# Two-layer hybrid mixer on one core: HGRN's masks on ScalarE, branch outputs by features, modulation blocks under mLSTM's gates

## The reference

```python
mod = silu(c) @ w_mod[l] + b_mod[l]                 # shift, scale, gain; 24 column blocks
o_a = softmax attention of MLA
o_b = two-way gated linear attention (HGRN):  scores[t,s] = sum_k q[t,k] k[s,k] prod(f[s+1..t,k])
o_c = mLSTM, two-way, with exponential gates and a maximum for stability
o_d = retention: q, k turned by a rotary table, scores * gamma^|t-s|, two-way
outs = [o_a, rms_norm(o_b)*silu(g_b), rms_norm(o_c)*sigmoid(g_c), rms_norm(o_d)*silu(g_d)]
acc  = sum_n sigmoid(gate_n) * (outs[n] @ w_branch[n]);   x = x + g1 * (acc @ w_out)
x    = x + g2 * (relu(h @ w_ff1)**2 @ w_ff2)
```

## Time and profile before

| | us |
|---|---|
| three runs | 1765.21, 1768.84, 1768.99 (median 1768.84) |
| the profiled execution | 1768.83, its span 1767.0 |
| TensorE busy | 1639.5 (93%), 9934 matmul records |
| VectorE, ScalarE, POOL busy | 862.8, 688.5, 263.8 |
| mean granted TensorE clock | 0.965 of full |

### The profile page before, as it was taken

One profiled execution on the slowest core, in us unless ns is written; L12 is line 12 of the kernel. 1 busy time (PEld: TensorE's weight loads), 2 busy tenths in 40 slices (PEclk: granted clock), 3 DMA queues, 4 the chain that ended last, 5 costly groups with the idle time before them and its releaser, 6 DMA issues.

```text
span 1767.0 us, 23662 instructions
## 1 busy us (share of the span) xinstructions
PE 1639.5 (93%) x9934; PEld 1347.5 (76%) x9934; DVE 862.8 (49%) x1283; ACT 688.5 (39%) x970; POOL 263.8 (15%) x193
## 2 busy tenths in 40 slices
PE   5987899999999999889999999878899989989998
PEld 3776686775667768667777777677788777989998
DVE  4399425554363325532223223469456554566553
ACT  5510223343635423433113322350345466455452
POOL 0044001230121110022002200012002230203030
PEclk9998999999999999899999999888999999989999
DMA  8331233212221143244443444221231322445552
GB/s 337 109 130 49 73 126 113 93 74 65 85 78 60 55 155 108 83 167 167 167 157 139 157 167 143 85 88 45 95 128 69 123 76 94 146 149 201 181 191 96
DMA packets 36442, 213.02 MB, mean 121 GB/s; under 512 B 3888, under 2 KB 7344, under 8 KB 12656
## 3 DMA queue, kind: packets, MB, share of 16 engines
q1 hardware_dynamic: 36336, 211.50, 33.3%
HBM read 209.39 MB, written 2.10 MB: 120 GB/s over the span
## 4 chain that ended last, share of the span: by engine, by line
PE 81%; DVE 11%; ACT 5%; issue 2%; DMA 1%; SPq 0%; DVEq 0%; ACTq 0%
PE ps L971 10%; PE ps L973 9%; PE ps L972 9%; PE ps L527 9%; PE ps L529 8%; PE ps L528 8%; PE ps L505 5%; DVE arena L1785 5%; PE ps L772 3%; PE ps L582 2%; PE ps L802 2%; PE ps L841 2%; DVE parts L1627 2%; DVE arena L1754 1%; PE ps L638 1%
## 5 line engine op out<-in xcount | busy, mean ns | idle before, releaser
L527 PE MATMUL ps<-parts,whi 128*128 128x512 f32 (+1 forms) x928 | 334.0, 360 | 7.1 <-issue 3.0
L529 PE MATMUL ps<-parts 128*128 128x512 f32 (+1 forms) x960 | 331.2, 345 | 0.0
L973 PE MATMUL ps<-parts 128*128 128x512 f32 (+1 forms) x960 | 323.3, 337 | 0.0
L528 PE MATMUL ps<-parts,whi 128*128 128x512 f32 (+1 forms) x928 | 320.7, 346 | 0.0
L971 PE MATMUL ps<-parts 128*128 128x512 f32 (+1 forms) x928 | 315.0, 339 | 0.0
L972 PE MATMUL ps<-parts 128*128 128x512 f32 (+1 forms) x928 | 312.5, 337 | 0.0
L1653 DVE TENSOR_TENSOR parts<-ring,parts 128x1024 fp32r<-128x1024 f32 x124 | 147.6, 1232 | 248.8 <-ACT parts L1246 248.8
L1627 DVE TENSOR_TENSOR parts<-ring,whi 128x1024 fp32r<-128x1024 f32 (+1 forms) x136 | 174.1, 1322 | 134.3 <-ACT whi L1216 134.2
L1246 ACT ACTIVATE parts<-ring 128x1024 fp32r<-128x1024 f32 x124 | 124.4, 1050 | 264.0 <-PE ps L973 251.8
L1216 ACT ACTIVATE whi<-ring 128x1024 fp32r<-128x1024 f32 (+1 forms) x136 | 134.7, 1041 | 210.0 <-DMA ring<-in_w_in 98.0
L527 PEld LDWEIGHTS ps<-parts,whi 128*128 128x128 f32 x928 | 177.5, 191 | 43.2 <-issue 21.4
(11 more groups left out here) (255 smaller groups left out, 2221.0 us busy)
## 6 DMA issues: line engine op xcount, KB each, us to landing
ring<-in_w_ff SPq DMA_DIRECT2D x64, 1024.0 KB, 4.8
ring<-in_w_in SPq DMA_DIRECT2D x60, 1024.0 KB, 5.0
ring<-in_w_mod SPq DMA_DIRECT2D x40, 1024.0 KB, 4.8
arena<-in_w_mod SPq DMA_DIRECT2D x8, 1024.0 KB, 20.8
ring<-in_w_branch SPq DMA_DIRECT2D x32, 256.0 KB, 5.2
ring<-in_w_out SPq DMA_DIRECT2D x8, 1024.0 KB, 4.8
arena<-in_tables_rt SPq DMA_DIRECT2D x2, 1280.0 KB, 7.7
X<-in_x SPq DMA_DIRECT2D x2, 1024.0 KB, 7.8
```

The source lines that it names most:

```text
L527: pe.matmul(ps[0:m, 0:n], w_hi[:, k, c], x_hi[:, k, 0:n], start=(k == 0), stop=False)
L528: pe.matmul(ps[0:m, 0:n], w_hi[:, k, c], x_lo[:, k, 0:n], start=False, stop=False)
L529: last = pe.matmul(ps[0:m, 0:n], w_lo[:, k, c], x_hi[:, k, 0:n], start=False, stop=(k == KD - 1))
L973: last = pe.matmul(ps[:, 0:nt], w_lo[:, k, c], x_hi[:, k, 0:nt], start=False, stop=(k == kt - 1))
```

## The change

In layer 0 the modulation blocks that ran behind hg, mq, mk and mv run behind mLSTM's merge tiles; HGRN's gates take blocks 12 to 15 and mLSTM's 16 to 19, `PACKS` follows. mLSTM's 16 gate columns are loaded into the tail of mo's slot. POOL's `masks` go: ScalarE copies the wanted halves and writes zeros to the others. Queries of level 2L are scaled before the keys of level L. Values become weights (64 wide), scores move, heads 2j and 2j+1 go to the two halves of the columns, and the result has features in partitions; the norms of HGRN and retention are sums by a matrix of ones, Ln and Exp; MLA's sums are spread by products with the identity. mLSTM keeps the old way (`branch_tokens`). Retention works on pairs of heads, with one buffer for the backward decays (`RDB`), and its decays 2 and 3 move ahead on ScalarE and POOL. The products across 128 alternate between the halves of the rows.

The core of the diff:

```diff
-    return [("mod", 0, {HG: 16, MLA: 20}[n] + j)] if n in (HG, MLA) else []
...
-IN_EXTRA = ("hq", "hv", "hg", "mq", "mk", "mv", "rq", "rk")
...
-PACKS = [(0, 8, 8), (0, 16, 4), (0, 20, 4), (1, 0, 8), (1, 8, 8), (1, 16, 8)]
+    return [("mod", 0, {HG: 12, ML: 16, MLA: 20}[n] + j)] if n != RT else []
...
+IN_EXTRA = ("hq", "hv", "rq", "rk")
...
+PACKS = [(0, 8, 4), (0, 12, 8), (0, 20, 4), (1, 0, 8), (1, 8, 8), (1, 16, 8)]
...
-                return [(0, KD * (b - a), io["w_in"][l, :, KD * a:KD * b])]
+                last = [(2048, 2048 + KD * 16, io["w_in"][l, :, KD * b:KD * (b + 16)])] if key[2] == "mo" else []
+                return [(0, KD * (b - a), io["w_in"][l, :, KD * a:KD * b])] + last
...
-                    last.then_inc(*product.up(("o", HG, l, g)))
-
...
+                for j in range(2):
+                    ps = bank(("o", HG, l, j), fixed=j)
+                    for i in range(2 * rounds):
+                        for step in range(16 // (2 * rounds)):
+                            t, k = divmod(done, KD)
+                            if k == 0:
+                                pv = bank(("rv", l, t))
+                            value_step(l, "rv", t, k, pv)
+                            done += 1
+                        if i + j == 0:
+                            pe.wait_ge(*s_hx.at(("x256", l, 3)))
+                            pe.wait_ge(*s_hp.at(("pt", l, 64, 3 if l == 0 else 1)))
+                        other = i + 1 - 2 * (i % 2)
+                        blocks = [(PT[:, :, i, :], i), (XP1[:, :, other * P:(other + 1) * P], other)]
+                        if i < 2:
+                            blocks += [(XP2[:, :, s * 256 + i * P:s * 256 + (i + 1) * P], 2 + s) for s in range(2)]
+                        last = weigh_pair(ps[:, i * P:(i + 1) * P], j, blocks, HV)
+                    last.then_inc(*product.up(("o", HG, l, j)))
+
+            def weigh_pair(o, j, blocks, values):
+
+                for n, (scores, s) in enumerate(blocks):
+                    for e in range(2):
+                        h = 2 * j + e
+                        last = pe.matmul(o[64 * e:64 * e + 64], values[:, s, h * HD:(h + 1) * HD], scores[:, h],
+                                         start=(n == 0), stop=(n == len(blocks) - 1))
                 return last
+
+            def branch_sum(n, l, j):
+
+                nt = T if l == 0 else LAT
+                pe.wait_ge(*s_oa.at(("osq", n, l, j)))
+                ps = bank(("os", n, l, j))
+                for e in range(2):
+                    r = slice(64 * e, 64 * e + 64)
+                    last = pe.matmul(ps[r, 0:nt], tab("ones")[r, 0:64], SQ[r, j, 0:nt], start=True, stop=True)
+                last.then_inc(*product.up(("os", n, l, j)))
...
+            def retention_scores(l, j):
+
+                for b in range(3 if l == 0 else 2):
+                    pair = [bank(("rqk", l, 2 * j + e, b)) for e in range(2)]
+                    q0 = LAT if b == 2 else 0
+                    for i in range(2):
+                        s = i if b == 0 else 2 + i
+                        for e, ps in enumerate(pair):
+                            r = slice(64 * e, 64 * e + 64)
+                            last = pe.matmul(ps[:, i * 256:(i + 1) * 256], RK[r, j, s * P:(s + 1) * P], RQ[r, j, q0:q0 + LAT],
+                                             start=True, stop=True)
+                            if i:
+                                last.then_inc(*product.up(("rqk", l, 2 * j + e, b)))
...
-                            last.then_inc(*product.up(("ro", l, h)))
-                    mla_turn(l, *divmod(h, 2))
+                retention_scores(l, 0)
+                merge(l, ML, [6])
+                retention_values(l, 0)
+                for j in range(2):
+                    mla_turn(l, 1, j)
...
+            def mla_spread(l):
+
+                pe.wait_ge(*s_av.at(("asum", l)))
+                for j in range(2):
+                    ps = bank(("rb", l, j))
+                    for t in range(4 if l == 0 else 2):
+                        g, i = divmod(t, 2)
+                        for e in range(2):
+                            c = 4 * i + 2 * j + e
+                            last = pe.matmul(ps[64 * e:64 * e + 64, t * P:(t + 1) * P],
+                                             asum[:, g, c:c + 1].broadcast_to([P, HD]), tab("ident"), start=True, stop=True)
+                    last.then_inc(*product.up(("rb", l, j)))
...
-                for g in rounds:
-                    branch_turn(HG, l, g)
+                    if j == 0:
+                        for i in range(2):
+                            branch_sum(HG, l, i)
...
+            def mask_zeros(l, L):
+
+                i = LEVELS.index(L)
+                for g in range(2 if l == 0 else 1):
+                    if L > 2:
+                        act.wait_ge(*product.at(("hl", l, L // 4, 2 * g + 1)))
+                    for rows, side in ((FW, 0), (BW, 1)):
+                        v = halves(QS[i % 2], rows, g * LAT, (g + 1) * LAT, L, side)
+                        z = zero4[rows, 0:1].unsqueeze(2).broadcast_to([64, HEADS, P // L]) if L == 1 else \
+                            zero4[rows, 0:1].unsqueeze(2).unsqueeze(3).broadcast_to([64, HEADS, P // L, L])
+                        act.activation(v, z, ACT.Copy)
+
+            def mask(l, L):
+
+                i = LEVELS.index(L)
+                act.wait_ge(*s_hd.at(("decq", l, L)))
+                for g in range(2 if l == 0 else 1):
+                    for rows, side in ((FW, 1), (BW, 0)):
+                        v, q = [halves(x, rows, g * LAT, (g + 1) * LAT, L, side) for x in (QS[i % 2], QT)]
+                        last = act.activation(v, q, ACT.Copy)
...
+                    ps = read(act, ("o", n, l, j))
+                    act.activation(SQ[:, j, 0:nt], ps[:, 0:nt], ACT.Square, scale=HD ** -0.5)\
+                        .then_inc(*s_oa.up(("osq", n, l, j)))
+                if n == HG:
+                    part_high(l, ("gate", HG, 0))
+                for j in range(2):
+                    ps = read(act, ("os", n, l, j))
+                    freed(("os", n, l, j), "branch_raw", ("oln", n, l, j))
+                    act.activation(RS[:, j, 0:nt], ps[:, 0:nt], ACT.Ln, bias=tab("eps")).then_inc(*s_oa.up(("oln", n, l, j)))
+                for j in range(2):
+                    act.wait_ge(*s_oa.at(("oln", n, l, j)))
+                    act.activation(RS[:, j, 0:nt], RS[:, j, 0:nt], ACT.Exp, scale=-0.5).then_inc(*s_oa.up(("ort", n, l, j)))
...
-                elif h >= 2:
-                    act.wait_ge(*s_rv.at(("prob", l, h - 2)))
-                for d, far in enumerate((RADF, RADB)):
-                    act.activation(RD[h % 2][d], far, ACT.Exp, scale=lgam(l, d, h)).then_inc(*s_ra.up(("e", l, h, d)))
...
+                for d, (far, e) in enumerate(((RADF, RD[h]), (RADB, RDB))):
+                    if h and d:
+                        act.wait_ge(*s_rp.at(("d", l, h - 1)))
+                    act.activation(e, far, ACT.Exp, scale=lgam(l, d, h)).then_inc(*s_ra.up(("e", l, h, d)))
...
+                retention_decay(l, 2)
...
                         merge(l, ML, [2, 3])
...
+            def query_decay(l, L):
+
+                nq = T if l == 0 and L < 128 else LAT
                 if L < 128:
                     dve.wait_ge(*s_hm.at(("mask", l, L, 1 if l == 0 else 0)))
                 else:
                     dve.wait_ge(*product.at(("h128", l, 1, 1)))
...
+                dve.wait_ge(*s_hd.at(("decq", l, L)))
+                if L > 1:
+                    dve.wait_ge(*s_hd.at(("gate", l, L)))
+                scale(QT, FW, 0, nq, L, 1)
+                scale(QT, BW, 0, nq, L, 0).then_inc(*s_hd.up(("decq", l, 2 * L)))
+
+            def key_decay(l, L):
+
+                if L < 128:
+                    dve.wait_ge(*product.at(("hl", l, L, 3 if l == 0 else 1)))
                 if L > 1:
...
+                for j in range(2):
+                    dve.wait_ge(*s_oa.at(("ort", n, l, j)))
+                    freed(("o", n, l, j), "branch_normed", ("on", n, l, j))
+                    dve.scalar_tensor_tensor(out=RS[:, j, 0:nt], in0=bank_of(("o", n, l, j))[:, 0:nt], scalar=gain,
+                                             in1=RS[:, j, 0:nt], op0=ALU.mult, op1=ALU.mult)\
+                        .then_inc(*s_ov.up(("on", n, l, j)))
+                if n == HG:
+                    part_low(l, ("gate", n, 0))
+                for j in range(2):
+                    dve.wait_ge(*s_ov.at(("on", n, l, j)))
+                    dve.wait_ge(*s_pa.at((name, l, 1)))
+                    dve.tensor_tensor(OUT[:, n % 2, j, 0:nt], RS[:, j, 0:nt], gate[:, j, 0:nt], ALU.mult)\
+                        .then_inc(*s_og.up(("og", n, l, j)))
...
-                    if h:
-                        mla_turn(l, *divmod(h - 1, 2))
-                mla_turn(l, 1, 1)
+                merge(l, ML, [5])
+                for j in range(2):
```

(76 more changed lines are left out.)

341 lines of the change are left out of this document (140 added, 201 removed).

## The result

The changed kernel takes 1747.95 us (median of four runs, 1744.10 to 1750.91) against 1767.22 for the kernel before, a ratio of 0.9884 with a 95% interval of 0.9864 to 0.9903. So it is faster, by 1.2%, clear of the scatter: by 19 us in the medians and by 22.8 in the profiled executions (1746.02 against 1768.83, spans 1744.2 and 1767.0), where 53.8 were forecast. 1715.0 was wrong, and so was the range, which ended at 1740.

A forecast was written before the change was run, and what follows sets the result against it. TensorE, busy 93% of the span, was taken as the bound, with VectorE's scalings holding the ladder; gains of 56.0 less 2.2 for small tiles gave 53.8 off 1768.8, so 1715.0 us, range 1703 to 1740.

The forecast's parts named there:

- The ring's look-ahead: Under mLSTM's gates: loads shortened by the moved blocks cost nothing, over 8 us against loads of 4.8; blocks themselves -4.3 us.
- a wait for loads under mLSTM's gates: Listed sign that would make the forecast wrong, in mLSTM's stage; given no size.
- The ladder: HGRN's levels: masks off POOL end its slowing of VectorE's key scalings; 22.5 us gained in layer 0, 10.9 in layer 1.
- Values by features: Value products in overlapping half-array pairs: HGRN +7.8 us, retention and MLA +8.8 each before walking their stages.
- rival (b): Tiles don't overlap, so values, scores, sums and spread lose 42.2 us: 1757; chance 0.07.
- Branch sums: Norm sums by a matrix of ones, 5.2 us added; in layer 0 a pair takes 0.86 us.
- Rival (a): Sums' two row halves writing one bank run one after another, costing 5.2 us more: 1720; chance 0.12.
- New waits: HGRN's gates wait longer for a bank held until VectorE copies mLSTM's rows, -3.8 us; layer 1's mLSTM branch -3.2.
- the wait for decay 2: Layer 1: decay 2 with two table loads comes before gate 1's sigmoid on ScalarE, within a term of -3.2 us.
- Retention and MLA: Walked stages: first RT gate earlier by 7.8 us in layer 0 and 8.4 in layer 1; MLA +9.9.
- (c): More waits than walked, through ScalarE and the rotating banks: six stages each lose 2.5 us more, 1730; chance 0.08.

The follow-up runs named there:

- experiment 1: Changed kernel with modulation block 16 loaded and multiplied behind the second kv projection instead of behind mLSTM's gate block 0; 1725.88 us, ratio 0.9769.
- experiment 3: Kernel before with only the four modulation blocks moved out of HGRN's ladder, masks still on POOL, values by tokens; 1774.38 us, ratio 1.0028.
- experiment 2: Changed kernel with all modulation blocks back where the kernel before has them, eight in HGRN's ladder, none under mLSTM's gates; 1739.47 us, ratio 0.9844.
- experiment 10: Changed kernel with HGRN's value products in half as many groups, each twice as long; one run, 1747.57 us.
- experiment 6: Kernel with block 16 behind kv, and retention's decay 2 moved behind mLSTM's gate 1 on ScalarE and POOL; 1729.93 us, ratio 0.9774.
- experiment 5: Changed kernel with mq's high part made on ScalarE ahead of the first mask and level 2's zeros; 1740.26 us, ratio 0.9828.
- experiment 8: Changed kernel with block 16 behind kv, mLSTM's rows copied first, mq's high part first, decay 2 late, second hg filler behind level 1; 1711.00 us, ratio 0.9677.

## Why the prediction was wrong, step by step

**The ring's look-ahead** ("between those products and the need lie over 8 us against loads of 4.8, so nothing") is the step that failed. The stretch lost 22.1 us instead of 4.3, 17.8 of the 31 that are missing in all, and undoing the one block made the profiled execution 20.9 us shorter, some 18 of them by this wait and what it drew after it. I had found that gate block 1 now waits for the last product of gate block 0, and measured the time to its own product on TensorE. But the first to need a load is ScalarE, which makes the high part, and it does so early: at 384.7 in experiment 1. Behind it in the same queue stand the roots that TensorE needs next. What had to be priced was not the distance from load to product but everything queued behind the instruction that waits. The sentence on "a wait for loads under mLSTM's gates", among the things that would make me wrong, named the place without a price.

**The ladder.** The mechanism was right and experiment 3 shows it: POOL's contention set the ladder's pace, and its price was 3.8 us a scaling. The size was too large, 17.7 instead of 22.5 and 8.0 instead of 10.9. ScalarE's four copies take 2.55 to 2.74 us, 0.64 to 0.69 each and not 0.5 to 0.55: I took the row of a copy out of PSUM without strides, and which of the two matters no run shows. The last cross products begin 93.5 us after level 0, not 87.1 as walked. Of these 6.4 us, 2.5 are the low clock in some of the stalls, by experiment 1, and 1.1 are mq's low part, which was done 16.9 us after level 0 and not 15.9. ScalarE and VectorE there:

```profile
96.41 2.64 ACT L1288 ACTIVATE arena<-zero 64x512 f32<-64x512 f32 x4
99.06 2.01 ACT L1275 ACTIVATE whi<-ring 128x1024 fp32r<-128x1024 f32 x2
```

```profile
100.15 2.36 DVE L1722 TENSOR_TENSOR parts<-ring,whi 128x1024 fp32r<-128x1024 f32 x2 [6.51 <-ACT whi L1275]
102.43 2.45 DVE L1864 TENSOR_TENSOR arena<-arena 64x1024 f32<-64x1024 f32 x2
```

The last scaling then waits 3.13 us for TensorE's products of level 64, a wait that I had not walked; it is 1.49 in experiment 1, so 1.6 of it belongs to the 2.5 above. 1.7 us came back behind: the last cross products took 3.37 us from start to start, where they ran at the low clock before (5.05, granted clock 0.66). I had also booked the blocks' leaving at nothing for the ladder. In the sum that was harmless, but by experiment 2 the whole gain hangs on it: masks on ScalarE alone would have gained 0.5 us in layer 0 and not 22.5, so that this term came near is in part luck.

**Values by features.** The tiles overlap, and rival (b) is out: four pairs of 256 columns take 1.88 us start to start, 0.43 a pair and one entry of 0.16. HGRN's term was mis-sized (5.0 instead of 7.8), because twelve groups between value steps lose 0.33 each by experiment 10, 4.0 us, where I had allowed 1.0.

**Branch sums.** Rival (a) is out as well. Two pairs of 512 columns, different row halves and one bank for each pair, in layer 0 of the kernel after:

```profile
244.16 1.93 PE L790 MATMUL ps<-SQ,tf 64*64 64x512 f32 x8
```

The next product starts at 246.03, so a pair costs 0.93 us and not 1.7. The rule of the Trainium skill ("TensorEngine Tiling (Array Packing)", section "Gotcha 1: PSUM Pressure") that spoke for this rival doesn't show here; the measurement decides.

**New waits.** HGRN's gates lost 4.8 instead of 3.8. The wait itself was right (2.63 and 3.72 us for the copy of the rows). In layer 0 TensorE then ran five products of the first gate at 0.23 us and the next eight at 0.43; in layer 1 most of that gate ran at the low clock too (4.45 us instead of 2.95). The branch of layer 1 lost 4.1 instead of 3.2: the wait for decay 2 was right and experiment 6 took it away, 2.8 us with its cold stretch.

**Retention and MLA.** Layer 1's walk was exact (8.4), with a wait of 3.59 us in it, the first scores' for a bank that VectorE's gate product held. Layer 0's fell short by 3.0 after block 19's 1.07 us: waits of 1.08, 0.87, 0.91 and 2.41 us where I had 1.2, 1.1 and 1.7, and merge 6's gate, which ran partly at the low clock (7.15 us instead of 5.6). MLA gained 7.2 instead of 9.9: its values gave 4.6 and 3.2 (5.3 and 3.5 forecast), its first gate at the low clock (6.67 us instead of 5.6) took 1.1 back, and the last 0.6 us I can't place.

**The chances.** Of the cases with a place of their own none was this one. (c), more waits, was the nearest in kind, with 2.5 us for each stage and 8 in 100; the real one was a single wait of 11.7 us and what it drew after it. (Forecast and (a) to (c) add up to 0.97, where I wrote 0.96.)

## What to carry to other kernels

When a step is inserted into a ring of loads, find for each load that now starts later the first engine that waits for it, and price everything in that engine's queue behind the wait, not the distance to the product that uses the load. Two parts of a change can be worth nothing alone and 15 us together (here masks off POOL, and loads out of ScalarE's way), so a step whose cover is another engine's wait must be priced with the other steps made and not made. And where half-array pairs stand between full products, make the groups long.

## What the runs showed of the hardware that was not expected

The granted clock fell in stretches in which TensorE was never idle. From 340 to 360 us, both kernels in mLSTM's stage with the same code, experiment 2 and then the changed kernel (span, busy time of PE, PEld, DVE, ACT, POOL, clock, DMA share, GB/s):

```profile
340.00:360.00 20.00, 20.00 (x79) 14.22 (x79) 10.81 (x26) 7.38 (x7) 5.23 (x5) 0.70 0.03 12
```

```profile
340.00:360.00 20.00, 19.97 (x105) 15.77 (x104) 12.92 (x31) 10.10 (x11) 6.77 (x7) 1.00 0.32 119
```

Over mLSTM's stage the low clock made experiment 2's profile some 10 us and experiment 5's 16 us longer than the changed kernel's, in a stage that their edits don't touch. Most of the tighter kernels scatter more than the kernel before (experiment 5 from 1733.10 to 1751.83, against 1765.21 to 1768.99; not experiment 8, from 1710.44 to 1712.32), and their edits had to be read from stretches of the trace, not from totals. What brings the low clock on no run here shows. Nor does the same wait always bring it: behind the first HGRN gate's wait of 2.63 us in layer 0 the changed kernel lost 1.6 us, experiment 1 nothing; it lost 1.4 us some 20 us later, in a gate with no wait before it (from 275.37, 7.01 us instead of 5.57).
